# FFN down projection of a diffusion-transformer layer as seven block products, in three rounds of inner tiles

## The reference

```
x = x + gate1 * ( (sig(gA) * (oA @ w_pa) + sig(gB) * (oB @ w_pb)) @ w_out )
x = x + gate2 * SwiGLU(RMSNorm(x) * (1 + scale2) + shift2)

def swiglu(h, w1, w3, w2):
    return (jax.nn.silu(h @ w1) * (h @ w3)) @ w2
```

## Time and profile before

| what | us |
|---|---|
| median of 3 runs | 1395.66 (1395.28 to 1397.66) |
| profiled execution, its span | 1395.5 |
| PE busy | 1360.4 (97%) |
| DVE busy | 811.8 (58%) |
| ACT busy | 672.1 (48%) |
| POOL busy | 218.0 (16%) |

### The profile page before, as it was taken

One profiled execution on the slowest core, in us unless ns is written; L12 is line 12 of the kernel. 1 busy time (PEld: TensorE's weight loads), 2 busy tenths in 40 slices (PEclk: granted clock), 3 DMA queues, 4 the chain that ended last, 5 costly groups with the idle time before them and its releaser, 6 DMA issues.

```text
span 1395.5 us, 26273 instructions
## 1 busy us (share of the span) xinstructions
PE 1360.4 (97%) x10442; PEld 1270.9 (91%) x10442; DVE 811.8 (58%) x1739; ACT 672.1 (48%) x1480; POOL 218.0 (16%) x189
## 2 busy tenths in 40 slices
PE   6999999999999999999999999899999999999998
PEld 4798989989998998999897888899999999999998
DVE  6466655665565566556536566657966434766422
ACT  4463736446373644637356555337655312555321
POOL 1011020202002020200032220000344003444000
PEclk7999999999999999999999999999999999999999
DMA  9643533233333323313326223522232332332332
GB/s 305 204 133 89 154 95 112 56 100 107 90 108 95 104 63 112 96 59 114 119 83 219 69 69 123 165 76 61 61 91 62 104 89 65 92 91 62 84 91 68
DMA packets 202560, 144.49 MB, mean 104 GB/s; under 512 B 8719, under 2 KB 188215, under 8 KB 202183
## 3 DMA queue, kind: packets, MB, share of 16 engines
q1 hardware_dynamic: 202439, 142.82, 34.7%
HBM read 126.77 MB, written 17.99 MB: 104 GB/s over the span
## 4 chain that ended last, share of the span: by engine, by line
PE 91%; ACT 3%; SPq 2%; DMA 2%; issue 1%; DVE 1%; DVEq 0%; ACTq 0%
PE ps L1195 31%; PE ps L1730 17%; PE ps L1767 11%; PE ps L1494 8%; PE ps L1421 2%; PE ps L1717 2%; PE ps L1626 2%; PE ps L1365 1%; PE ps L1428 1%; PE ps L1341 1%; PE ps L1371 1%; PE ps L1594 1%; PE ps L1269 1%; PE ps L1696 1%; PE ps L1440 1%
## 5 line engine op out<-in xcount | busy, mean ns | idle before, releaser
L1195 PE MATMUL ps<-hT_r,WAH_r 128*128 128x320 f32 x912 | 229.0, 332 | 6.4 <-ACT zs L2063 2.4
L1195 PE MATMUL ps<-xT_r,WAH_r 128*128 128x320 f32 x912 | 208.1, 309 | 0.0
L1195 PEld LDWEIGHTS ps<-hT_r,WAH_r 128*128 128x128 f32 x912 | 145.5, 190 | 26.1 <-issue 10.1
L1195 PEld LDWEIGHTS ps<-xT_r,WAH_r 128*128 128x128 f32 x912 | 153.2, 189 | 0.0
L1195 PE MATMUL ps<-hT_r,W_r 128*128 128x320 f32 x592 | 134.2, 310 | 0.0
L1767 PE MATMUL ps<-a_part,W_r 128*128 128x320 f32 x704 | 132.3, 310 | 0.0
L3170 POOL TENSOR_TENSOR gm<-sqkq,dt 128x1280 f32<-128x1280 f32 x8 | 23.5, 2934 | 571.8 <-DVE Xc L2655 499.8
L1767 PEld LDWEIGHTS ps<-a_part,W_r 128*128 128x128 f32 x704 | 110.3, 188 | 0.0
L1730 PE MATMUL ps<-t_big_r,W_r 128*128 128x320 f32 x380 | 107.2, 310 | 0.5 <-ACT naT L2320 0.4
L1730 PE MATMUL ps<-b_part,W_r 128*128 128x320 f32 x456 | 101.3, 309 | 0.0
L1195 PEld LDWEIGHTS ps<-hT_r,W_r 128*128 128x128 f32 x592 | 99.6, 190 | 0.0
(11 more groups left out here) (436 smaller groups left out, 3275.4 us busy)
## 6 DMA issues: line engine op xcount, KB each, us to landing
oT<-in_ffn_w SPq DMA_DIRECT2D x44, 512.0 KB, 5.3
W<-in_w_in SPq DMA_DIRECT2D x36, 512.0 KB, 4.1
WAH<-in_w_ada SPq DMA_DIRECT2D x18, 1024.0 KB, 6.9
naT<-in_w_in SPq DMA_DIRECT2D x24, 512.0 KB, 4.2
oT<-in_ffn_w SPq DMA_DIRECT2D x16, 704.0 KB, 4.7
ext_dram<-naT SPq DMA_DIRECT2D x28, 320.0 KB, 4.1
tA<-ext_dram SPq DMA_DIRECT2D x16, 320.0 KB, 3.6
GCB<-gc_dram SPq DMA_DIRECT2D x7, 640.0 KB, 4.6
```

The source lines that it names most:

```text
L1195: m = e.matmul(ps[:, bank + b, 0:n], w[:, k, :], x[:, k, a:a + n], start=k == 0 and i == 0, stop=k == KD - 1 and i == 2, skip_group_check= ...
```

## The change

The down projection is built like the up projection. The program becomes a list of 34 turns n: hidden tiles 0 to 7, four down turns, tiles 8 to 15, four down turns, tiles 16 to 21, four down turns (ROUNDS, TURNS). Turn 0 to 7 are tiles 0 to 7, turn 8 is the first down turn, and so on.

A down turn (q, g) makes both column tiles of group g over the 8 inner tiles of its round (6 in the last round) by seven products, with the same names, banks and weight slots as an up turn. Its blocks of weights are: column tile s against inner tiles of even or odd place. A product has 4 x 3 = 12 matmuls, in the last round 3 x 3 = 9. So 12 down turns have 8 x 84 + 4 x 63 = 924 matmuls, where 16 steps had 1056. The other operand is made of the hidden rows. With B11, B12 the halves of an even tile and B21, B22 those of the next odd tile, VectorE makes D1 = B12 - B11, D2 = B22 - D1, D3 = B22 - B12 and D4 = B21 - D2 (`sum_down`), and B11, D1, D2, B21, D3, B22, D4 are each split into a big part by ScalarE (`hid_big`) and a small part by VectorE (`hid_small`), 320 columns each. Per two tiles there were two splits of 640 columns.

Each partial result is added into the residual at once (`result`, seven steps, 10 or 11 instructions per down turn: y11a after P1, y22b after P5, y12a after P6, y11b after P2, y22a after P7, y12b after P3, y21 after P4). PE waits for y11a before P6, for y12a before P7, for y22a before P4. GpSimd makes weight sums in down turns too. In the last round PE turns both rows of group g - 1 after P1 of group g, and both rows of the last group at the end; the rows are turned out of xT.

```diff
-            def down(q, g, s):
-                wait(dve_ff, f"down {q} {g} {s}")
...
-                for k in range(KH):
...
-                    for n, (w, xp) in enumerate(((w_big_down[s][:, k, :], 0), (w_big_down[s][:, k, :], 1), (w_small_r[3 * s + k // 4][:, k % 4, :], 0))):
-                        for b, (a, c) in enumerate(HALVES):
+            def down(n):
+
+                q, g = TURNS[n][1]
+                a, f, x = 6 + n % 2, 2, 3
+                read_by(n - 2, "hid", "y21")
+                product(n, "A11", a, True)
+                if q == len(ROUNDS) - 1 and g:
+                    for s in range(2):
+                        turn_y(g - 1, s)
+                read_by(n - 1, "C12", "y12b")
+                product(n, "S1", x, True)
+                wait(dve_ff, f"y11a {n}")
+                product(n, "S2", a, False)
+                read_by(n - 1, "C11", "y11b")
+                product(n, "A12", f, True)
+                wait(dve_ff, f"y12a {n}")
+                product(n, "S3", a, False)
+                wait(dve_ff, f"y22b {n}")
+                product(n, "S4", x, False)
+                wait(dve_ff, f"y22a {n}")
+                product(n, "A22", a, False)
```

VectorE's loop over the turns:

```diff
+            for n in range(FIRST, LAST + 1):
+                if n - 1 in UPS:
+                    for d in ("B11", "D1") if even(n - 1) else ("B21", "D3", "B22", "D4"):
+                        hid_small(n - 1, d)
+                if n in UPS:
+                    plain_small(n + 1, "A11")
+                    sum_up("C11", n)
+                    sum_small(n + 1, "S1")
+                    sum_up("C22", n)
+                    plain_small(n + 1, "A12")
+                    sum_up("C12", n)
+                    hidden(1, n)
+                    if even(n):
+                        sum_small(n + 1, "S2")
+                        hidden(0, n)
+                        sum_down(n, "D1")
                     else:
...
+                        sum_down(n, "D2")
+                        sum_down(n, "D3")
+                        sum_small(n + 1, "S2")
+                        hid_small(n, "D2")
+                        hidden(0, n)
+                        sum_down(n, "D4")
+                    sum_small(n + 1, "S3")
+                    sum_small(n + 1, "S4")
+                    plain_small(n + 1, "A22")
+                    continue
+                result(n, "y11a")
```

The start of the FFN on ScalarE (turns 0 to 3) changes in this way:

```diff
-    names += ["S1 3", "S2 3", "silu 2", "A12 3", "S3 3", "hid 2", "S4 3", "A22 3"]
...
+    names += ["silu 1", "A11 3", "D2 1", "B21 1", "S1 3", "S2 3", "D3 1", "B22 1", "D4 1", "silu 2", "A12 3", "S3 3", "B11 2", "S4 3", "A22 3", "D1 2"]
```

and that on VectorE:

```diff
-    names += ["hid 0", "T1", "A12 2", "A22 2", "lo 0", "T2", "hid 1", "A11 3", "lo 1", "T3", "S1 3", "S2 3", "hid 2", "A12 3", "S3 3", "T4", "S4 3", "A22 3"]
+    names += ["hid 0", "sum D1 0", "T1", "A12 2", "A22 2", "B11 0", "D1 0", "T2", "hid 1", "sum D2 1", "sum D3 1", "A11 3", "D2 1", "B21 1", "sum D4 1", "T3", "S1 3", "S2 3"]
+    names += ["D3 1", "B22 1", "D4 1", "hid 2", "sum D1 2", "A12 3", "S3 3", "T4", "S4 3", "A22 3"]
```

More of the change, by code:

```diff
@@ new lines, in dve_ff_steps @@
+    names += ["D3 1", "B22 1", "D4 1", "hid 2", "sum D1 2", "A12 3", "S3 3", "T4", "S4 3", "A22 3"]
+    late = ["B11 2", "D1 2"]
+    for n in range(FIRST, LAST + 1):
+        names += late
+        late = []
+        more = [f"{o} {n + 1}" for o in OPERANDS] if n < LAST else []
+        w = dict(zip(OPERANDS, more))
+        if TURNS[n][0] == "up":
+            names += [w["A11"], f"C11 {n}", w["S1"], f"C22 {n}", w["A12"], f"C12 {n}", f"hid1 {n}"]
+            if even(n):
+                names += [w["S2"], f"hid {n}", f"sum D1 {n}"]
+                late = [f"B11 {n}", f"D1 {n}"]
+            else:
+                names += [f"sum D2 {n}", f"sum D3 {n}", w["S2"], f"D2 {n}", f"hid {n}", f"sum D4 {n}"]
+                late = [f"B21 {n}", f"D3 {n}", f"B22 {n}", f"D4 {n}"]
+            names += [w["S3"], w["S4"], w["A22"]]
+            continue
+        for done, o in (("y11a", "A11"), ("y22b", None), ("y12a", "S1"), ("y11b", "A12"), ("y22a", None), ("y12b", "S2"), (None, "S3"), ("y21", "S4"), (None, "A22")):
+            names += [f"{done} {n}"] if done else []
+            names += [w[o]] if o in w else []
@@ L1755, in down @@
[L1755 to L1768 removed]
+                part = x_part
@@ new lines, in product @@
+                if TURNS[n][0] == "down":
+                    part = down_part
+                    if TURNS[n][1][1] == 0:
+                        d = next(d for d in D_OF if D_OF[d] == o)
+                        wait(dve_ff, f"{d} {last_of_kind(n, d not in ('B11', 'D1'))}")
+                wait(dve_ff, f"{o} {n}")
+                half = tiles_half(n)
+                for k in range(half):
+                    for j, (w, x) in enumerate(((w_big, part[0]), (w_big, part[1]), (w_small_r, part[0]))):
+                        m = e.matmul(ps[:, bank, 0:HT], w[i][:, k, :], x[i][:, k, :], start=start and k == 0 and j == 0, stop=k == half - 1 and j == 2, skip_group_check=True)
@@ L2418, in _ @@
+            for s in range(2):
+                y_out(GD - 1, s)
         @block.vector
```

558 lines of the change are left out of this document (256 added, 302 removed).

## The result

| | before | after |
|---|---|---|
| median of 4 runs each, us | 1395.68 | 1407.19 |
| lowest to highest | 1395.28 to 1397.66 | 1406.96 to 1410.36 |
| profiled span, us | 1395.5 | 1408.3 |
| matmuls | 10442 | 10310 |

The ratio is 1.0091, with a 95% interval of 1.0079 to 1.0104: the kernel is 0.9% slower, although it has 132 matmuls fewer, as counted beforehand. The prediction was 1400.5 us with a range of 1389 to 1407. The sign is right, the time lies 6.7 us above the forecast and 0.2 us above the range.

A forecast was written before the change was run, and what follows sets the result against it. PE was taken to bound the kernel, busy 1360.4 of 1395.5 us. The terms -19.4 - 0.5 - 0.6 + 3.1 + 13.8 + 3.3 + 5.1 gave +4.8, with 0.2 for the median 1400.5 us, range 1389 to 1407.

The forecast's parts named there:

- 132 matmuls: All down turns: 924 matmuls in place of 1056, at 0.1467 us each on PE: -19.4 us.
- border: From first down projection to up turns: weights prepared one turn ahead, so two slow products of 12 matmuls go: -0.5 us.
- end: From the last result's start to the last turning on PE: about 0.6 us in place of 1.19: -0.6 us.
- snap1 after an odd tile, 7: Odd tile before a further tile: P6 late by 0.44 us, as ScalarE needs VectorE's sum D4; seven times, +3.1 us.
- y11a, 3: First down turn of each round: P6 waits 4.6 us for y11a, behind VectorE's small parts and late splits; +13.8 us.
- start of the FFN: Turn 3, once: added VectorE work delays the second hidden row, P6 starts at 1003.05; +3.3 us, bounds 2 and 5.
- clock: After each of three stalls before down turns PE's clock falls, 1.7 us each: +5.1 us, bounds 0 and 7.
- slack of 0.3 us: Down turns other than the first of a round: y11a done at 15.25, due 15.6, so no stall.
- case (e): Slower: GpSimd's S4 and the results clash in each down turn, 9 x 0.7 = 6.3 us more, 1406.8 us; chance 0.15.
- (b): Stalls as forecast, but PE's clock does not fall: 1395.4 us, no change; chance 0.18.
- (c): Shorter stalls, 3 x 3.5 us before down turns, no clock fall: 1387.9 us, 1391.5 with half the deviations; chance 0.18.
- (d): VectorE's queue never holds PE for long, gain whole but for a microsecond or two: 1376 to 1378 us; chance 0.07.

## Why the prediction was right or wrong, point by point

Against its own steps, in us, on the profiled spans (+12.8):

| step | forecast | measured | by |
|---|---|---|---|
| 132 matmuls | -19.4 | -19.4 | instruction count, 0.1467 each |
| border | -0.5 | -0.5 | no such pieces in the chain of after |
| end | -0.6 | about -0.3 | below |
| snap1 after an odd tile, 7 | +3.1 | +7.8 | pair of turns 25.76 against 24.64 |
| y11a, 3 | +13.8 | +13.6 | P6 late by 4.57, 4.57, 4.48 |
| start of the FFN | +3.3 | +3.8 | P6 of turn 3 at 1003.56, before 999.80 |
| clock | +5.1 | +8.3 | four pieces above |

The measured column adds up to 13.3; 0.5 are rounding and what the pieces miss.

- **The gain** is right. So is the end: the last result starts at 1402.75 and the last turning at 1403.35, 0.60 as forecast; what follows it took 0.3 longer.
- **y11a** is right in its mechanism, its place and its size. The instructions came where the list put them: sum D4 at t = 14.68 (complete 15.20 forecast, 15.17 here), y11a at 19.58 (forecast 19.67), P6 at 20.17 (forecast 20.23). The run with GpSimd held measured the 1.1 us of contention by itself.
- **snap1 is the step that failed.** The prediction let ScalarE's D4 wait for VectorE's sum ("ScalarE needs the sum D4, complete at 14.72 + 0.48 = 15.20") and did not add up ScalarE's own list. That list has, from D2 on, eight instructions ahead of snap1, 5 x 0.36 and 3 x 0.52, which end at t = 16.26, while the sum is there at 15.2. P6 starts at 16.72 and not at 16.07: 1.12 us seven times in place of 0.44, beyond the bound of 0.7. With the prediction's own prices (5 x 0.33 and 3 x 0.51 from 12.89 on, then snap1) the same sum gives P6 at 16.6: 0.9 us of the 1.1 could have been read beforehand. The run with D3 and B22 behind snap1 shows that the 0.44 was right for VectorE and that ScalarE's queue was the rest. 4.7 of the 8.0 us by which the profiled execution lies above its forecast of 4.8 are here (between the medians it is 6.7).
- **The clock** was right in kind and too small. It fell a fourth time, at the start (2.8 us, which the prediction left to its upper bound), and the three others cost 1.5, 1.4 and 2.6 against 1.7 each. 3.2 us are here, in the profiled execution. The other three executions ran at a mean granted clock higher by 0.002 to 0.003, over 1405 us an estimated 2.8 to 4.2 us, and they were 3.1 to 3.4 us faster. So at the median the clock's term would be about 5, as forecast, and snap1 nearly the whole of the miss; no trace of those executions shows where the clock fell. The Trainium skill (TensorE: Matmul & The Clock Gate, Why this matters for your kernels) asks for no idle gaps between bursts. The run with the gaps filled agrees: the same wait, and 4.0 us less.
- **The start** is 0.5 above its estimate, within its bounds.
- **The nine other down turns** have no wait: the slack of 0.3 us held, and case (e) did not occur. The time of 1407 that it forecast was reached by another way, by a term that was 0.68 us too small in a place that occurs seven times, and by the clock.
- **The rivals** (b), clock holds, (c), shorter stalls, and (d), no stalls, are refuted by the rows above. Of what (d) hoped for, 31 us below the changed kernel, six rewritings of the lists brought 18.7.
- **What the prediction did not say** is how little a cure can be worth. It added the stalls up as separate terms; for the cost that was right, as the table shows, for a cure it isn't, since they are one queue: 13.6 us of waits for y11a gave back 4.1 when y11a was moved to the front, and over 20 us of waits moved at once gave back 2.4. The exception is the move by four splits only, which gave 5.9 us.

## What to carry to other kernels

When a step is added to a list, follow both lists that end in the same handover, the one that computes and the one that copies, up to the instruction that releases PE; the later of the two sums counts, and here an error of 0.7 us in a turn that repeats seven times is the largest one of the total. A queue in which several consumers wait has a deadline at each product: to move the first late instruction forward can make the second one late by nearly as much, so write down all due times, place everything, and read the next late one from the new trace; here that took six kernels, worth 0.6 to 6.9 us each, and turned 11.5 us behind into 7 us ahead. Saved matmuls count only as long as the engines that feed PE have the slack; look at their busy share in the stages concerned, not over the span.
